# A layer on one Trainium2 core: VectorE's work in the 64 attention steps dealt out in another order, w_ada's rows mostly in the first 24 steps, the end of the stage reordered, half of x loaded again by SyncE

## The chip, the cores and the metric

The kernel runs on one core of one Trainium2 chip. The metric is the device time of one execution in microseconds (us); the figure compared is the median over runs. The engines have short names in all rows: PE is TensorE's matmul, PEld its weight load, DVE is VectorE, ACT is ScalarE, POOL is GpSimd and SP is SyncE, which here only issues DMAs. Every engine runs its own instructions in the order in which they are written, and waits on semaphores of the others.

## The reference

One transformer layer over 1024 tokens of width 1024, in f32. What matters here, cut short:

```python
mod = silu(c) @ w_ada + b_ada          # six parts of 1024: shift, scale, gate, twice
h = rmsnorm(x, g_mix) * (1 + scale) + shift
q, k, v, q_idx, k_idx, w_idx, u = split(h @ w_in)
# index attention, in query blocks of 128: every token takes its 256 best keys
score = sum_h w_idx[h] * relu(q_idx[h] . k_idx)      # causal
sel = top_k(score, 256)
o = softmax(q . k[sel] / 8) @ v[sel]                 # 8 heads of 64, 2 kv heads
# conformer branch: 31-tap depthwise convolution of 512 channels, layernorm over channels, silu
y = silu(layernorm(conv31(glu(u)) + conv_b) * norm_g + norm_b)
x = x + gate1 * (concat(o, y) @ w_out)
x = x + gate2 * mlp(rmsnorm(x) * (1 + scale2) + shift2)
out = rmsnorm(x, g_final)
```

## The kernel before

Each f32 matmul is made as three rounded ones (high x high, low x high, high x low), so nearly every operand is split into a `_hi` and a `_lo` part. The execution has this order: norm and first parts of `w_ada`; the projections with `w_in`; index scores; then the **attention stage**, which this change is about (338 to 707 us of the profiled execution); `w_out` (to 796 us); the MLP, over half of the whole time, which the change does not touch.

The attention stage is 64 **steps**, n = 8t + i for query block t (128 tokens) and head i. One list, `MICRO`, is written out by hand as Python tables, and all engines run through that same list, each taking from it what is its own. So the list sets the order on every engine. Per step there are: `scores` (PE, two heads at a time, matmuls into one of two banks), `mask` (DVE, adds the mask or the index selection and takes the maximum, line 1521 and two small rows behind it), `exp` (ACT), `turn` (PE transposes the probabilities, ACT copies them, line 1002), `values` (PE). PE's scores of a pair of heads overwrite the banks of the pair before and wait for its masks (line 2012 waits for line 1521). Once per query block: `invert` and `spread` (reciprocal of the softmax sums, turned by PE), `divide` (DVE, line 1558, frees the bank of `values`: PE's line 2090 of the next block waits for it), `out_hi` (ACT, line 1022) and `out_lo` (DVE, line 1561) which split the block's output.

Dealt out among these steps is other work:

- `topk` for query tile 4 (DVE, pairs at lines 1385 and 1387, steps 0 to 30). For tiles 5 to 7 the 256th best score is found by a search in rounds instead: `sel_pass` (ACT counts the scores above a candidate with three Sign activations, line 949), then `sel_step` (DVE, four small operations on 128x3 at lines 1406 to 1416, which give the next candidate). Rounds lie in steps 0 to 31 with n % 4 < 3; the pass of step n is answered by the `sel_step` of step n + 1. `sel_fin` (DVE, lines 1436 to 1454) finishes each tile in 6 steps between 32 and 51.
- convolution taps on PE, whose diagonal matrices POOL builds.
- the convolution's layernorm for the first 512 tokens (half 0), lines 1568 to 1594 on DVE and 1035 to 1048 on ACT: centre, square, sum (PE), root, reciprocal, scale, affine, sigmoid (`ln_gate`), silu, and the split `ln_hi` and `ln_lo`. Half 1 lies at the end of the stage.
- 32 rows of `w_ada` (`ada`, DVE, line 1542 or 1545): one 128x1024 operation each, from a buffer `raw` that SP fills. SP has 4 such buffers and issues the transfer for slot n when slot n - 4 has been used. The sums are needed by `modsum` (step 46) and `gate` (steps 57 and 58).
- at steps 60 and 62 and after the stage POOL splits the rows of `w_out` into high and low (lines 593 and 595).

Behind the stage, PE runs `w_out` in units: first on attention output and conv half 0 for tokens 0 to 511 (`mixed` in the list), then for the other 512 tokens, for which it needs `out_lo` of block 7 and then `ln_lo` of half 1. DVE adds the result to x (`mixed1`, lines 1608 and 1610), and ACT issues the DMAs that load x again.

## Time and profile before

| what | value |
|---|---|
| median of 3 runs | 2895.67 us |
| all runs | 2901.35, 2895.67, 2895.38 us |
| the profiled execution | 2891.27 us |
| its span, first to last instruction | 2889.5 us |
| mean granted clock of PE | 0.973 |
| PE busy | 2692.2 us, 93% of the span |
| DVE busy | 1673.8 us, 58% |
| POOL busy | 1148.5 us, 40% |
| ACT busy | 764.8 us, 26% |
| attention stage, starts of its steps | 0: 338.0, 8: 377.5, 16: 421.3, 24: 464.2, 32: 513.7, 48: 611.7, 63: 690.6 us |

Times are read from the start of the span. A step starts where its row of line 1521 starts on DVE. The profiled execution is 4.4 us below the median of the runs. Busy shares are averages over stages with different limits, so the stages are read one by one.

### The profile page before, as it was taken

The page shows a single profiled execution, that of the slowest core. Times are in us where ns is not written, and L with a number is a line of the kernel's source. Part 1 is how long each engine was busy: PE and PEld are TensorE (multiplying, and loading weights), DVE is VectorE, ACT ScalarE, POOL GpSimd, SP SyncE. Part 2 cuts the span into 40 slices and gives each one's busy share as a digit, 9 for nine tenths or more (in the row PEclk, how much of TensorE's full clock was granted, in tenths as well). Part 3 has the DMA queues.
Part 4 walks back from the last instruction along what each step waited for, and adds up shares of the span by engine and source line. Part 5 has one row for each costly group of instructions (what it writes and reads, how often), then busy time and mean ns, then how long its engine had stood idle before and what let it go on. Part 6 is the DMA issues. An engine that isn't in the chain of part 4 may idle for free.

```text
span 2889.5 us, 34826 instructions
## 1 busy us (share of the span) xinstructions
PE 2692.2 (93%) x13584; PEld 2213.7 (77%) x13584; DVE 1673.8 (58%) x2150; ACT 764.8 (26%) x1322; POOL 1148.5 (40%) x764
## 2 busy tenths in 40 slices
PE   4999898899999999999999999788799999999998
PEld 4867776677878888888877777677688888888887
DVE  6278988854666566566585782455526334444335
ACT  4235477434231001111023442222214100111002
POOL 2422464533554344344342223333264334334332
PEclk8999999999999999999999999999999999999999
DMA  6201111111411111111122110000221111111111
GB/s 217 66 12 34 36 61 58 59 38 36 147 59 46 42 58 46 41 58 44 48 73 73 37 37 15 1 1 1 87 95 59 39 49 58 37 50 58 36 51 59
DMA packets 142490, 153.35 MB, mean 53 GB/s; under 512 B 7183, under 2 KB 105252, under 8 KB 142374
## 3 DMA queue, kind: packets, MB, share of 16 engines
q1 hardware_dynamic: 136512, 141.87, 15.5%
q10 hardware_dynamic: 5862, 9.89, 1.0%
q8 instruction: 78, 1.28, 0.2%
q14 instruction: 38, 0.31, 0.0%
HBM read 143.35 MB, written 8.39 MB: 53 GB/s over the span
## 4 chain that ended last, share of the span: by engine, by line
PE 78%; DVE 13%; ACT 4%; issue 3%; DMA 1%; POOL 1%; ACTq 0%; SPq 0%; DVEq 0%; POOLq 0%
PE ps L1936 11%; PE ps L1921 11%; PE ps L1937 11%; PE ps L1938 11%; PE ps L1922 11%; PE ps L1923 11%; PE ps L2318 3%; PE ps L2012 2%; DVE yt L1758 2%; ACT sel_out L949 1%; PE ps L2090 1%; DVE yt L1747 1%; DVE score L1387 1%; PE ps L2116 1%; DVE best L1385 1%
## 5 line engine op out<-in xcount | busy, mean ns | idle before, releaser
L1921 PE MATMUL ps<-h_hi,w_hi 128*128 128x512 f32 x1472 | 585.4, 398 | 10.1 <-issue 5.6
L1922 PE MATMUL ps<-h_lo,w_hi 128*128 128x512 f32 x1472 | 575.6, 391 | 0.0
L1923 PE MATMUL ps<-h_hi,w_lo 128*128 128x512 f32 x1472 | 575.3, 391 | 0.0
L696 POOL TENSOR_TENSOR w_hi<-raw,zero 128x1024 fp32r<-128x1024 f32 x128 | 243.7, 1904 | 781.0 <-PE ps L1923 398.0
L1936 PE MATMUL ps<-w_hi,u_hi 128*128 128x512 f32 x1024 | 399.2, 390 | 0.0
L1937 PE MATMUL ps<-w_lo,u_hi 128*128 128x512 f32 x1024 | 399.1, 390 | 0.0
L1938 PE MATMUL ps<-w_hi,u_lo 128*128 128x512 f32 x1024 | 398.9, 390 | 0.0
L1078 ACT ACTIVATE act_r<-ps 128x512 f32<-128x512 f32 x128 | 76.5, 598 | 1131.4 <-PE ps L1923 1131.4
L1642 DVE TENSOR_TENSOR act_r<-act_r 128x512 f32<-128x512 f32 x128 | 166.0, 1297 | 330.4 <-ACT act_r L1078 330.4
L699 POOL TENSOR_TENSOR w_lo<-raw,w_hi 128x1024 fp32r<-128x1024 f32 x128 | 338.1, 2641 | 10.0
L1921 PEld LDWEIGHTS ps<-h_hi,w_hi 128*128 128x128 f32 x1472 | 278.0, 189 | 77.2 <-issue 17.0
L1922 PEld LDWEIGHTS ps<-h_lo,w_hi 128*128 128x128 f32 x1472 | 278.1, 189 | 59.9 <-issue 3.7
L1923 PEld LDWEIGHTS ps<-h_hi,w_lo 128*128 128x128 f32 x1472 | 277.9, 189 | 58.6
L1647 DVE TENSOR_TENSOR u_lo<-act_r,u_hi 128x512 fp32r<-128x512 f32 x128 | 226.8, 1781 | 0.0
L1936 PEld LDWEIGHTS ps<-w_hi,u_hi 128*128 128x128 f32 x1024 | 192.7, 188 | 40.0
L1938 PEld LDWEIGHTS ps<-w_hi,u_lo 128*128 128x128 f32 x1024 | 192.7, 188 | 40.0
L1937 PEld LDWEIGHTS ps<-w_lo,u_hi 128*128 128x128 f32 x1024 | 192.7, 188 | 40.0
L1655 DVE TENSOR_TENSOR x<-x,ps 128x512 f32<-128x512 f32 x128 | 88.0, 687 | 212.2 <-PE ps L1938 212.2
L1936 PE MATMUL ps<-w_hi,h_hi 128*128 128x512 f32 (+2 forms) x512 | 184.0, 359 | 18.2 <-DVE h_lo L1862 6.7
L1937 PE MATMUL ps<-w_lo,h_hi 128*128 128x512 f32 (+2 forms) x512 | 182.7, 357 | 0.0
L1938 PE MATMUL ps<-w_hi,h_lo 128*128 128x512 f32 (+2 forms) x512 | 182.3, 356 | 0.0
L1662 DVE TENSOR_TENSOR x<-x,tmp 128x512 f32<-128x512 f32 x128 | 155.0, 1211 | 4.4
(421 smaller groups left out, 4158.4 us busy)
## 6 DMA issues: line engine op xcount, KB each, us to landing
raw<-in_w_up_dram SPq DMA_DIRECT2D x64, 512.0 KB, 4.0
raw<-in_w_down_dram SPq DMA_DIRECT2D x64, 512.0 KB, 3.2
raw<-in_w_ada_dram SPq DMA_DIRECT2D x48, 512.0 KB, 3.7
raw<-in_w_in_dram SPq DMA_DIRECT2D x32, 512.0 KB, 3.7
raw<-in_w_out_dram SPq DMA_DIRECT2D x32, 512.0 KB, 3.3
x<-in_x_dram SPq DMA_DIRECT2D x8, 512.0 KB, 10.7
x<-in_x_dram ACTq DMA_DIRECT2D x8, 512.0 KB, 9.4
x_mid<-x SPq DMA_DIRECT2D x8, 512.0 KB, 5.4
```

What stands on the lines that cost most here:

```text
L696: g_.tensor_tensor(w_hi[:, r, :], raw[:, r, :], zero.to_broadcast([P, 1024]), ALU.add).then_inc(sem("w_hi_done"), 1)
L699: g_.tensor_tensor(w_lo[:, r, :], raw[:, r, :], w_hi[:, r, :].bitcast(F32), ALU.subtract).then_inc(sem("split_done"), 1)
L1642: v.tensor_tensor(act_r[:, b % 4, :], act_r[:, b % 4, :], act_r[:, b % 4, :], ALU.mult).then_inc(sem(f"u_sq{k}"), 1)
L1647: v.tensor_tensor(u_lo[c // 4][:, c % 4, :], act_r[:, c % 4, :], u_hi[c // 4][:, c % 4, :].bitcast(F32), ALU.subtract).then_inc(sem(f"u_lo ...
L1655: v.tensor_tensor(x[:, t, cols], x[:, t, cols], ps[:, n % 8, :], ALU.add).then_inc(sem(f"down_out{k}"), 1)
L1662: v.tensor_tensor(x[:, t, cols], x[:, t, cols], tmp2[:, n % 2, :], ALU.add).then_inc(sem(f"x_sum{k}"), 1)
L1921: mm(ps[:, bank, :], wh, h_hi[:, k, cols], start=(k == 0), stop=False)
L1922: mm(ps[:, bank, :], wh, h_lo[:, k, cols], start=False, stop=False)
L1923: last = mm(ps[:, bank, :], wl, h_hi[:, k, cols], start=False, stop=(k == NK - 1))
L1936: mm(o, hi[:, k0 + k, tok], wh, start=(start and k == 0), stop=False)
L1937: mm(o, hi[:, k0 + k, tok], wl, start=False, stop=False)
L1938: last = mm(o, lo[:, k0 + k, tok], wh, start=False, stop=(stop and k == 1))
```

## The change

Nothing is computed otherwise; instructions stand elsewhere in the engines' orders.

- **w_ada's rows** (`ADA_SLOTS`): before one row at steps 0, 1, 3, 4, 6, 8, 9, 11 and so on, to 49 (32 rows); now one in each of steps 0 to 23, then 25, 28, 39, 45, 46, 53, 54, 55.
- **divide, out_hi, out_lo** of block t - 1: from steps 8t + 3, 8t + 3, 8t + 4 to steps 8t + 2, 8t + 2, 8t + 3. On ACT `out_hi` then stands ahead of the three Sign activations of its step.
- **layernorm of half 0**: its four columns are dealt out over more steps (centre over 26 and 27, scale one each in 33 to 36, affine over 37 and 38, silu one each in 40 to 43); its reciprocal goes from 31 to 32.
- **sel_fin**: each tile one step later.
- **end of the stage, half 1**: square behind step 63's `exp`; sum, root later; reciprocal, scale and affine from before `invert` to behind `out_lo` of block 7.
- **x**: tiles 0 to 3 are loaded by SP, behind the transfer of the slot N_FIRST - 12 and a wait for the last scores (ahead of the later `w_out` slots), tiles 4 to 7 by ACT as before.

```diff
--- before.py
+++ after.py
@@ -399,7 +399,7 @@
         SEL_EARLY, SEL_ROUNDS = 8, 4
         SEL_AT = {n: SEL_EARLY + k for k, n in enumerate(n for n in range(32) if n % 4 < 3)}
         FIN_SLOTS = {}
-        for ti, at_slots in zip(SEL_TILES, (range(32, 38), range(39, 45), range(46, 52))):
+        for ti, at_slots in zip(SEL_TILES, (range(33, 39), range(40, 46), range(47, 53))):
             for part, n in enumerate(at_slots):
                 FIN_SLOTS[n] = [("sel_fin", ti, part)]
         UNIT_SLOTS = (0, 6, 12, 18, 24, 34, 42, 52, 62)
@@ -412,13 +412,17 @@
             return CONV_K * u + -(-CONV_K * (n - n0) // (n1 - n0))
 
         LN_BANK = (1, 7)
-        LN_SLOTS = {26: [("ln_mean", 0)], 28: [("ln_square", 0)], 29: [("ln_sum", 0)], 30: [("ln_root", 0)],
-                    31: [("ln_recip", 0)], 34: [("ln_scale", 0)], 37: [("ln_affine", 0)], 39: [("ln_gate", 0)],
-                    42: [("ln_silu", 0)], 62: [("ln_mean", 1), ("ln_square", 1)],
-                    63: [("ln_sum", 1), ("ln_root", 1), ("ln_recip", 1), ("ln_scale", 1), ("ln_affine", 1)]}
+        LN_SLOTS = {26: [("ln_mean", 0, 0), ("ln_center", 0, 0), ("ln_center", 0, 1)],
+                    27: [("ln_center", 0, 2), ("ln_center", 0, 3)],
+                    28: [("ln_square", 0, 0)], 29: [("ln_sum", 0, 0)], 30: [("ln_root", 0, 0)], 32: [("ln_recip", 0, 0)],
+                    33: [("ln_scale", 0, 0)], 34: [("ln_scale", 0, 1)], 35: [("ln_scale", 0, 2)], 36: [("ln_scale", 0, 3)],
+                    37: [("ln_affine", 0, 0), ("ln_affine", 0, 1)], 38: [("ln_affine", 0, 2), ("ln_affine", 0, 3)],
+                    39: [("ln_gate", 0, 0)], 40: [("ln_silu", 0, 0)], 41: [("ln_silu", 0, 1)], 42: [("ln_silu", 0, 2)],
+                    43: [("ln_silu", 0, 3)], 62: [("ln_mean", 1, 0)] + [("ln_center", 1, c) for c in range(NCC)],
+                    63: [("ln_square", 1, 0)]}
         HI_SLOTS = {44: 3, 46: 2, 54: 1, 62: 0}
         N_ADA = 4 * NK
-        ADA_SLOTS = {8 * i // 5: i for i in range(N_ADA)}
+        ADA_SLOTS = {n: i for i, n in enumerate(list(range(24)) + [25, 28, 39, 45, 46, 53, 54, 55])}
         GATE_SLOTS = {46: [("modsum", 0, 0)], 57: [("gate", 0, 0), ("gate", 0, 1)], 58: [("gate", 1, 0), ("gate", 1, 1)]}
         WSPLIT_SLOTS = {60: 0, 62: 1}
         MICRO = [("split_q", 0, 0), ("split_q", 1, 0)]
@@ -439,12 +443,12 @@
                     MICRO.append(("mask", t, i + e))
                     if n - 1 in SEL_AT:
                         MICRO.append(("sel_step", SEL_AT[n - 1], 0))
-                    if t and i + e == 4:
+                    if t and i + e == 2:
+                        MICRO.append(("divide", t - 1, 0))
+                    if t and i + e == 3:
                         MICRO.append(("out_lo", t - 1, 0))
                     if t and i + e == 0:
                         MICRO.append(("invert", t - 1, 0))
-                    if t and i + e == 3:
-                        MICRO.append(("divide", t - 1, 0))
                     if t and i + e == 1:
                         middle = (taps[1] + taps[2]) // 2
                         if middle > taps[1]:
@@ -457,11 +461,11 @@
                     if n in WSPLIT_SLOTS:
                         MICRO.append(("wsplit", WSPLIT_SLOTS[n], 0))
                     MICRO.append(("exp", t, i + e))
-                    if t and i + e == 3:
+                    if t and i + e == 2:
                         MICRO.append(("out_hi", t - 1, 0))
                     if n in HI_SLOTS:
                         MICRO += [("ln_hi", 0, HI_SLOTS[n]), ("ln_lo", 0, HI_SLOTS[n])]
-                    MICRO += [(kind, half, 0) for kind, half in LN_SLOTS.get(n, [])]
+                    MICRO += LN_SLOTS.get(n, [])
                     for ti, at_slots in TOPK_SLOTS.items():
                         if n in at_slots:
                             done, of = n - at_slots[0], len(at_slots)
...
-        MICRO += [("values", NT - 1, NH - 4), ("turn", NT - 1, NH - 2), ("mixed", 0, 0), ("turn", NT - 1, NH - 1),
-                  ("invert", NT - 1, 0), ("mixed", 0, 1), ("spread", NT - 1, 0), ("ln_gate", 1, 0), ("values", NT - 1, NH - 2), ("divide", NT - 1, 0),
-                  ("mixed", 0, 2), ("mixed", 0, 3), ("out_hi", NT - 1, 0), ("out_lo", NT - 1, 0), ("ln_silu", 1, 0)]
+        MICRO += [("values", NT - 1, NH - 4), ("turn", NT - 1, NH - 2), ("ln_sum", 1, 0), ("mixed", 0, 0),
+                  ("turn", NT - 1, NH - 1), ("invert", NT - 1, 0), ("ln_root", 1, 0), ("mixed", 0, 1), ("spread", NT - 1, 0),
+                  ("values", NT - 1, NH - 2), ("divide", NT - 1, 0), ("mixed", 0, 2), ("mixed", 0, 3), ("out_hi", NT - 1, 0),
+                  ("out_lo", NT - 1, 0), ("ln_recip", 1, 0)]
+        MICRO += [(kind, 1, c) for kind in ("ln_scale", "ln_affine") for c in range(NCC)] + [("ln_gate", 1, 0)]
+        MICRO += [("ln_silu", 1, c) for c in range(NCC)]
         MICRO += [("mixed", 1, t) for t in range(4)]
         MICRO += [(kind, 1, c) for c in reversed(range(NCC)) for kind in ("ln_hi", "ln_lo")]
 
...
+                if n == N_FIRST - 12:
+                    sp.wait_ge(sem("score_full"), NH * NT)
+                    for t in range(NT // 2):
+                        sp.dma_start(x[:, t, :], a["x"][0, t * P:(t + 1) * P, :]).then_inc(sem("x_in0"), 16)
 
             def mlp(k, n0, freed0, up, down):
 
@@ -1054,8 +1065,8 @@
 
             act.wait_ge(sem("attn_lo"), NT)
             act.wait_ge(sem("ln_silu"), 2 * NCC)
-            for t in range(NT):
-                act.dma_start(x[:, t, :], a["x"][0, t * P:(t + 1) * P, :]).then_inc(sem(f"x_in{t // 4}"), 16)
+            for t in range(NT // 2, NT):
+                act.dma_start(x[:, t, :], a["x"][0, t * P:(t + 1) * P, :]).then_inc(sem("x_in1"), 16)
 
             act.dma_start(frow, a["g_final"].rearrange("(o d) -> o d", o=1).to_broadcast([P, D])).then_inc(sem("frow_in"), 16)
 
@@ -1567,28 +1578,24 @@
                                          vec[:, m0 + 3 * NK:m0 + 5 * NK], ALU.add))
                     v.scalar_tensor_tensor(scl[:, 1, :], mod[:, 4 * NK:5 * NK], 1.0, vcols("g_mlp"), ALU.add,
                                            ALU.mult).then_inc(sem("scale_ready"), 1)
-                if kind == "ln_mean":
+                if kind == "ln_center":
                     dve.wait_ge(sem("ln_mean"), t + 1)
-                    for c in range(NCC):
-                        v.scalar_tensor_tensor(conv[:, c, cols], ps[:, LN_BANK[t], :], -1.0 / CONV_CH, conv[:, c, cols],
-                                               ALU.mult, ALU.add).then_inc(sem("ln_cent"), 1)
+                    v.scalar_tensor_tensor(conv[:, i, cols], ps[:, LN_BANK[t], :], -1.0 / CONV_CH, conv[:, i, cols],
+                                           ALU.mult, ALU.add).then_inc(sem("ln_cent"), 1)
                 if kind == "ln_recip":
                     dve.wait_ge(sem("ln_sd"), t + 1)
                     link(v.reciprocal(tmp2[:, 1, :], tmp2[:, 1, :]))
...
```

The first place is DVE in step 11, the fourth step of query block 1. Before:

```order
L1521 ISA prob,smax<-ps,cmask 128x256
L1521 ISA smax 128x1
L1528 TENSOR_SCALAR snm<-smax 128x1
L1406 TENSOR_TENSOR sel_acc<-sel_sum,sel_rank 128x3
L1407 TENSOR_TENSOR sel_pick<-sel_acc,sel_cand 128x3
L1408 TENSOR_TENSOR sel_low<-sel_low,sel_pick 128x3
L1416 SCALAR_TENSOR_TENSOR sel_cand<-sel_base,sel_low 128x3
L1558 TENSOR_TENSOR otok<-ps,otok 128x512
L1385 MAX best<-score_161 128x8
L1387 MATCH_REPLACE score_161<-best,score_161 128x640
L1542 SCALAR_TENSOR_TENSOR gate_sum_174<-raw,csil,gate_sum_174 128x1024
L1521 ISA prob,smax<-ps,cmask 128x256
```

And now:

```order
L1532 ISA prob,smax<-ps,cmask 128x256
L1532 ISA smax 128x1
L1539 TENSOR_SCALAR snm<-smax 128x1
L1417 TENSOR_TENSOR sel_acc<-sel_sum,sel_rank 128x3
L1418 TENSOR_TENSOR sel_pick<-sel_acc,sel_cand 128x3
L1419 TENSOR_TENSOR sel_low<-sel_low,sel_pick 128x3
L1427 SCALAR_TENSOR_TENSOR sel_cand<-sel_base,sel_low 128x3
L1569 TENSOR_TENSOR otok<-ps,otok 128x512
L1396 MAX best<-score_161 128x8
L1398 MATCH_REPLACE score_161<-best,score_161 128x640
L1553 SCALAR_TENSOR_TENSOR shift_sum<-raw,csil,shift_sum 128x1024
L1532 ISA prob,smax<-ps,cmask 128x256
```

The second of these begins at step 10's mask and ends at step 11's: `divide` (`otok<-ps,otok`) has gone from behind the small operations on 128x3 of step 11 to behind those of step 10, and the step has got a row of `w_ada` (`raw,csil`) as step 11 has.

The second place is ACT in step 10, the three Sign activations (`sel_out,sel_sum`) and the copy `h_hi<-otok`. Before:

```order
L1010 ACTIVATE prob,ssum<-prob,snm 128x256
L949 ACTIVATE sel_out,sel_sum<-score_162,sel_cand,sel_sign 128x768
L949 ACTIVATE sel_out,sel_sum<-score_163,sel_cand,sel_sign 128x896
L949 ACTIVATE sel_out,sel_sum<-score_164,sel_cand,sel_sign 128x1024
L1002 ACTIVATE probT<-ps 128x256
L1028 ACTIVATE conv<-ps,vec 128x512
L1010 ACTIVATE prob,ssum<-prob,snm 128x256
L1022 ACTIVATE h_hi<-otok 128x4x128
```

And now:

```order
L1021 ACTIVATE prob,ssum<-prob,snm 128x256
L1033 ACTIVATE h_hi<-otok 128x4x128
L960 ACTIVATE sel_out,sel_sum<-score_162,sel_cand,sel_sign 128x768
L960 ACTIVATE sel_out,sel_sum<-score_163,sel_cand,sel_sign 128x896
L960 ACTIVATE sel_out,sel_sum<-score_164,sel_cand,sel_sign 128x1024
L1013 ACTIVATE probT<-ps 128x256
L1039 ACTIVATE conv<-ps,vec 128x512
L1021 ACTIVATE prob,ssum<-prob,snm 128x256
```

The copy, which waits for DVE's `divide`, stood behind step 11's exp and now stands ahead of step 10's Sign activations.

The third place is DVE at steps 42 to 44, where block 4's output is divided, half 0's silu is made (`conv<-conv,squares`) and tile 6 is finished (`sel_out`, score_163). Before:

```order
L1590 TENSOR_TENSOR conv<-conv,squares 128x512 x4
L1447 TENSOR_SCALAR sel_out<-score_163,sel_kth 128x896
L1448 SCALAR_TENSOR_TENSOR sel_out<-ones,sel_out 128x896
L1521 ISA prob,smax<-ps,score_162 128x768
L1521 ISA smax 128x1
L1528 TENSOR_SCALAR snm<-smax 128x1
L1558 TENSOR_TENSOR otok<-ps,otok 128x512
L1450 TENSOR_SCALAR sel_out<-sel_out,sel_ties 128x896
L1451 SCALAR_TENSOR_TENSOR sel_out<-score_163,sel_kth,sel_out 128x896
L1542 SCALAR_TENSOR_TENSOR gate_sum_175<-raw,csil,gate_sum_175 128x1024
L1521 ISA prob,smax<-ps,score_162 128x768
```

And now:

```order
L1569 TENSOR_TENSOR otok<-ps,otok 128x512
L1597 TENSOR_TENSOR conv<-conv,squares 128x512
L1454 TENSOR_SCALAR sel_out<-score_163,sel_kth 128x896
L1455 TENSOR_REDUCE sel_higher<-sel_out 128x1
L1456 TENSOR_SCALAR sel_ties<-sel_higher 128x1
L1532 ISA prob,smax<-ps,score_162 128x768
L1532 ISA smax 128x1
L1539 TENSOR_SCALAR snm<-smax 128x1
L1572 TENSOR_TENSOR h_lo<-otok,h_hi 128x4x128
L1597 TENSOR_TENSOR conv<-conv,squares 128x512
L1458 TENSOR_SCALAR sel_out<-score_163,sel_kth 128x896
L1459 SCALAR_TENSOR_TENSOR sel_out<-ones,sel_out 128x896
```

Step 42 had four rows of silu and the first two rows of a part of `sel_fin`; now one silu row stands in each step, with one part of `sel_fin` and no row of `w_ada`.

The fourth place is DVE's end of the stage, behind the last mask. Before:

```order
L1528 TENSOR_SCALAR snm<-smax 128x1
L1577 RECIPROCAL tmp_151<-tmp_151 128x512
L1580 TENSOR_TENSOR conv<-conv,tmp_151 128x512 x4
L1585 TENSOR_SCALAR conv<-conv,vec 128x512 x4
L1554 RECIPROCAL srec<-ssum 128x8
L1558 TENSOR_TENSOR otok<-ps,otok 128x512
L1561 TENSOR_TENSOR h_lo<-otok,h_hi 128x4x128
L1590 TENSOR_TENSOR conv<-conv,squares 128x512 x4
L1594 TENSOR_TENSOR h_lo<-conv,h_hi 128x512 x4
```

And now:

```order
L1539 TENSOR_SCALAR snm<-smax 128x1
L1565 RECIPROCAL srec<-ssum 128x8
L1569 TENSOR_TENSOR otok<-ps,otok 128x512
L1572 TENSOR_TENSOR h_lo<-otok,h_hi 128x4x128
L1587 RECIPROCAL tmp_151<-tmp_151 128x512
L1589 TENSOR_TENSOR conv<-conv,tmp_151 128x512 x4
L1593 TENSOR_SCALAR conv<-conv,vec 128x512 x4
L1597 TENSOR_TENSOR conv<-conv,squares 128x512 x4
L1601 TENSOR_TENSOR h_lo<-conv,h_hi 128x512 x4
```

The reciprocal, scale and affine of half 1 stood ahead of the reciprocal of the softmax sums (`srec<-ssum`), and now stand behind `h_lo<-otok,h_hi`.

## Rows read from the trace of the kernel before

**Rows 1.** Windows: us; busy PE, PEld, DVE, ACT, POOL; granted clock; DMA share; GB/s.

```profile
338.00:464.20 126.20, 113.72 (x599) 87.44 (x598) 103.97 (x240) 89.51 (x187) 79.02 (x92) 0.93 0.20 63
464.20:508.40 44.20, 35.99 (x198) 25.13 (x196) 36.98 (x82) 36.16 (x67) 16.79 (x19) 0.93 0.15 49
508.40:679.60 171.20, 156.13 (x1117) 123.90 (x1117) 111.74 (x185) 73.24 (x143) 78.33 (x78) 0.94 0.14 44
679.60:705.10 25.50, 20.94 (x153) 14.73 (x154) 13.55 (x21) 13.27 (x22) 1.24 (x1) 0.97 0.06 22
705.10:800.80 95.70, 90.87 (x439) 75.66 (x437) 60.28 (x57) 28.81 (x46) 57.80 (x31) 0.98 0.36 127
```

**Rows 2.** Waits of PE, 338 to 708 us: us in total, times, longest.

```profile
PE ps L2012 <- DVE smax L1521: 25.6, 9, 5.0
PE ps L2090 <- DVE otok L1558: 6.1, 3, 3.3
PE ps L2098 <- DVE srec L1554: 2.3, 1, 2.3
PE ps L2135 <- ACT squares L1035: 2.2, 1, 2.2
```

**Rows 3.** The same view, 508.4 to 679.6 us.

```profile
PE ps L2012 <- DVE smax L1521: 19.4, 6, 5.0
```

**Rows 4.** Timeline of PE, three stalls: start, busy, row, in brackets the wait before.

```profile
508.37 0.79 PE L2012 MATMUL ps<-k_hi,q_hi 64*128 64x512 f32 x2 [5.03 <-DVE smax L1521]
...
576.96 0.76 PE L2012 MATMUL ps<-k_hi,q_hi 64*128 64x512 f32 x2 [4.97 <-DVE smax L1521]
...
591.05 0.80 PE L2012 MATMUL ps<-k_hi,q_hi 64*128 64x512 f32 x2 [4.07 <-DVE smax L1521]
```

**Rows 5.** Window behind the stall at 577 us, as in rows 1.

```profile
577.00:580.40 3.40, 3.40 (x24) 3.06 (x26) 3.33 (x4) 1.55 (x3) 0.22 (x1) 0.51 0.00 0
```

**Rows 6.** Timeline of DVE in steps 3 to 6.

```profile
357.26 1.28 DVE L1542 SCALAR_TENSOR_TENSOR gate_sum<-raw,csil,gate_sum 128x1024 f32<-128x1024 f32 x1
...
363.26 0.77 DVE L1406 TENSOR_TENSOR sel_acc<-sel_sum,sel_rank 128x3 f32<-128x3 f32 x1 [0.95 <-ACT sel_out L949]
...
369.75 0.70 DVE L1406 TENSOR_TENSOR sel_acc<-sel_sum,sel_rank 128x3 f32<-128x3 f32 x1 [1.63 <-ACT sel_out L949]
```

**Rows 7.** Timeline of ACT and DVE around steps 10 and 11.

```profile
389.81 1.03 ACT L949 ACTIVATE sel_out<-score,sel_cand,sel_sign 128x768 f32<-128x768 f32 x1 [0.66 <-DVE sel_cand L1416]
...
396.69 0.69 DVE L1558 TENSOR_TENSOR otok<-ps,otok 128x512 f32<-128x512 f32 x1
...
397.41 0.63 ACT L1022 ACTIVATE h_hi<-otok 128x512 fp32r<-128x512 f32 x1 [2.40 <-DVE otok L1558]
```

**Rows 8.** Groups of DVE by line, 338 to 508.4 us: busy, mean ns, idle before.

```profile
L1407 DVE TENSOR_TENSOR sel_pick<-sel_acc,sel_cand 128x3 f32<-128x3 f32 x23 | 11.4, 497 | 0.8
...
L1406 DVE TENSOR_TENSOR sel_acc<-sel_sum,sel_rank 128x3 f32<-128x3 f32 x24 | 7.4, 306 | 15.8 <-ACT sel_out L949 15.8
```

**Rows 9.** Timeline of DVE in steps 31 and 42.

```profile
510.34 3.35 DVE L1577 RECIPROCAL tmp<-tmp 128x512 f32<-128x512 f32 x1
...
567.67 3.77 DVE L1590 TENSOR_TENSOR conv<-conv,squares 128x512 f32<-128x512 f32 x4
```

**Rows 10.** Timeline of DVE and POOL behind the last mask.

```profile
698.85 2.50 DVE L1580 TENSOR_TENSOR conv<-conv,tmp 128x512 f32<-128x512 f32 x4
...
707.91 1.05 POOL L593 CAST w_hi<-raw 128x1024 fp32r<-128x1024 f32 x1 [27.06 <-PE ps L2090]
...
711.91 8.57 DVE L1590 TENSOR_TENSOR conv<-conv,squares 128x512 f32<-128x512 f32 x4
...
744.85 0.69 DVE L1608 TENSOR_TENSOR tmp<-ps,gate 128x512 f32<-128x512 f32 x1 [6.37 <-PE ps L1938]
```

**Rows 11.** DMA issues of the page: KB each, median us from issue to landing.

```profile
raw<-in_w_ada_dram SPq DMA_DIRECT2D x48, 512.0 KB, 3.7
...
x<-in_x_dram ACTq DMA_DIRECT2D x8, 512.0 KB, 9.4
```

19 lines of the change are left out of this document (8 added, 11 removed).

## Prediction

> **What bounds the kernel now.** I read the windows first, cut at the places where the stage changes its limit [rows 1]. From 338 to 464 us (steps 0 to 23) PE is busy 113.7 of 126.2 us, but DVE 104.0 and ACT 89.5 as well: none is full. In this stretch ACT and DVE hand the search for tiles 5 to 7 to each other: DVE waits 15.8 us in all for ACT's counts [rows 8], ACT waits for the next candidate (0.66 us, [rows 7]). That loop sets the pace; PE follows. From 464 to 508 us (steps 24 to 31) PE is busy 36.0 of 44.2 us, DVE 37.0. From 508 to 680 us PE is busy 156.1 of 171.2 us and DVE only 111.7: there PE is the bound, and what it loses is worth looking for. The end, 680 to 705 us, and `w_out` to 801 us are PE's too (90.9 of 95.7).
>
> The chain of losses is in the waits of PE [rows 2]: 25.6 us in nine waits of the scores for a mask. Of these 19.4 us in six waits lie from 508.4 us on [rows 3], but the first of the six is the one that ends at 508.37 (5.03 us, [rows 4]); so the PE-bound stretch itself holds 14.4 us in five, the largest 4.97 and 4.07 us [rows 4]. DVE has a mean load of 65% there, so the masks are late because single steps hold too much, not because DVE has too much work. A second loss is the clock. The stretch has a mean granted clock of 0.94 [rows 1], 10.3 us of 171.2. Right behind the stall of 4.97 us, from 577.0 to 580.4 us, the clock is 0.51, the 1.2 GHz level instead of 2.4, with PE busy all the time [rows 5]: 3.4 us there do 1.7 us of work. So a stall costs its own time and then 1.7 or 3.4 us more.
>
> The Trainium skill, "TensorE: Matmul & The Clock Gate" (Part 1), says that activity of PE is what keeps its fast clock and idleness what loses it; by this rule too removing stalls pays twice, and the trace agrees by the row of 0.51 behind the stall.
>
> **The change, step by step.** *Steps 0 to 23.* Nine rows of `w_ada` come in, 1.28 us each [rows 6]. Where a row stands in the step ahead, DVE waits 0.95 us for ACT's count, where none stands 1.63 us [rows 6]; a row of 1.28 us fits into the 1.63. This holds for the six steps 2, 5, 10, 13, 18 and 21: nothing. Steps 7 and 15 have no pass behind them, nothing waits there, and the row lies on the loop: 2.6 us. Step 23 likewise, 1.3 us, but PE's waits of about the same length that end there go (I take 1.1 off for lateness that PE already has). *Divide and out_hi.* ACT's copy takes 0.63 us and, ahead of the Sign activations of steps 10 and 18, waits for a `divide` of 0.69 us that follows DVE's small operations [rows 7]: about 1.3 us each time, 2.6 together. `divide` in one step and `out_lo` in the next take each other's place on DVE: nothing. That is 2.6 + 1.3 + 2.6 - 1.1 = 5.4; the loop has about 1.2 us of slack in these three periods, ACT's own 0.66 us wait [rows 7] being part of it, so I take **+4.2 us** at step 24, bounds 1.5 (only steps 7 and 15, a half hidden) and 15.4 (below). PE's 6.1 us of waits for `divide` [rows 2] lie inside this stretch and are worth nothing while the loop sets the pace.
>
> *Steps 24 to 31.* Rows leave steps 24, 27 and 30; that of step 30 stands directly ahead of mask 31, for which PE waits 5.03 us [rows 4]: **-1.3 us**. The third `out_hi` move (step 26) and centre cut in two take about as much as they give. So PE's scores of step 32 start at 508.4 + 4.2 - 1.3 = 511.3 us. A reciprocal of 3.35 us [rows 9] goes from ahead of mask 32 to ahead of mask 33, where PE has a pair of steps of 8 us or more to cover it.
>
> *Steps 32 to 61.* Before, single steps hold four silu rows, 3.77 us [rows 9], and behind them a part of `sel_fin` and a row of `w_ada`; the third place of the change shows them gone from one step into four. I laid the new order of DVE beside PE's own work per pair of steps (8 to 12 us at full clock, 171.2 - 14.4 - 10.3 = 146.5 in all): all masks but one come ahead of PE; the one of step 45 comes 1.8 us late, behind `sel_fin`'s last part and a row of `w_ada`. Left are this 1.8 us, 1.7 of clock behind it and 1.0 of clock behind the stall of step 31: 4.5 us instead of 24.7. **-20.2 us**, bounds -10 (half of the stalls stay as shorter ones that still cost the clock) and -24.
>
> *End of the stage.* Before, the reciprocal of 3.35 us and eight more rows stand ahead of `invert`, and PE waits 2.3 us for `srec` [rows 2]; now nothing stands there: -2.3. The 2.2 us wait for the squares [rows 2] moves with `ln_sum` behind more of PE's work, but the squares start behind step 63's `exp`: +0.3. Sum **-2.0**, bounds 0 and -4. The work moved behind `out_lo` runs beside POOL's splits, which start at 707.9 us, when `pv_done` comes [rows 10]. There four rows take 8.57 us, where four like them take 2.50 us alone [rows 10]. Priced so: reciprocal 3.4 [rows 9], scale, silu and lo 8.6 each, affine 2.5, together 31.7 us, from about 708 us on, with some 2 us of waits for the Sigmoids: DVE is through at 742 us on the clock of before. PE needs it for the second half of `w_out`, which by half of the last window [rows 1] begins at about 751; before, DVE had 6.4 us to spare ahead of 744.85 [rows 10]. With DVE's first `mixed1` rows between, it keeps 4 us or more. Cost nothing; without that cover up to 8 us.
>
> *DMAs.* A `w_ada` transfer takes 3.7 us, a tile of x 9.4 in the median [rows 11]. In steps 0 to 23 a row is used every 5.3 us with four buffers, so it lands in time. x's first half starts some 15 us earlier, on SP, with `w_out`'s slots behind it; PE wants the first of those only at about 715 us. Nothing.
>
> The sum: +4.2 - 1.3 - 20.2 - 2.0 = -19.3. The profiled execution of 2891.27 us would become 2872; it lies 4.4 us below the median of the runs, so against 2895.67 us I say **2876 us**.
>
> **The rivals.** *A: the rows land on the loop.* If DVE's wait for ACT doesn't take them up (a row in step n delays mask n + 1, that its exp, that the next pass), nine rows of 1.28 and three copies of 1.3 cost 15.4 us: 11.2 more, -8, **2888 us**. For it: ACT and DVE are both over 70% busy. Against it: a wait of 1.63 turned into 0.95 where a row stands. Chance 0.13. *B: the end of the stage pays.* All moved DVE rows at 2.14 us each (8.57/4) beside POOL, the reciprocal slowed as well, end about 8 us past PE's need: -11, **2884 us**. For it the 8.57 us; against it 4 us or more of slack. Chance 0.12. The Trainium skill, "SBUF — State Buffer", section "SBUF: two separate sides", says that VectorE and GpSimd share a port pair that one of them holds for a whole instruction. [...] *C, slower: the search's small rows.* In steps 0 to 31 the rows of line 1407 take 497 ns in the mean [rows 8], and single ones 0.16 or 0.77 [rows 6]: beside POOL they are five times as long. If the added DVE rows shift them so that all meet POOL's diagonals, a `sel_step` of four rows goes from 1.5 to 3.0 us, 24 times on the loop: +35, net +15, **2911 us**. It decides from 0.8 us per `sel_step`. Against it: POOL's order isn't changed, and 63% of its time there is busy already. Chance 0.06. *D: the stalls only move.* If DVE is late anyway through the 4.2 us by which steps 0 to 23 end later, or PE's waits shift to other masks with the clock as low, the stretch gains 5 instead of 20: about **2892 us**. Against it: 35% of DVE idle there, in long pieces. Chance 0.12.
>
> **How the numbers follow.** Chances: forecast 0.57, A 0.13, B 0.12, D 0.12, C 0.06. With its bounds the forecast covers 2868 to 2884. To hold eight in ten the range reaches from 2866 to 2891: it takes in A, B and most of the bounds, leaves out D's upper half and C. A difference under 0.2% (5.8 us) is about what this measurement can't tell from none. Faster by more (under 2889.9): forecast, B, most of A, a part of D: 0.80. Within: the rest of A and D, 0.13. Slower: C and a tail of D, 0.07.
>
> **What would show it.** Right: step 24 starts at 467 to 469 us; PE's waits for line 1521's successor from there to step 61 sum to under 4 us, and the clock of that stretch is 0.97 or more; scores of step 62 start 16 to 18 us earlier; no wait for `srec`; PE without a gap from there to 780 us. Wrong: step 24 at 475 or later (A), 490 (C); waits of PE for `h_lo` or `x` past 740 us (B); waits for masks above 10 us in new places (D). The number that I trust least is the +4.2, since it sums small terms of a loop of two engines.

## The result

The changed kernel takes 2890.44 us in the median of 20 runs (2885.75 to 2892.92), the kernel before 2897.46 in 20 runs (2891.8 to 2901.35): a ratio of 0.9976, with an interval of 0.997 to 0.9983, so 7 us faster. I had said 2876, almost 20 us faster. The profiled execution took 2888.07 us, with a span of 2886.3.

First the windows of the changed kernel, cut at the same steps as those of before [rows 1]:

```profile
338.00:471.50 133.50, 116.17 (x615) 87.75 (x613) 119.62 (x248) 89.19 (x187) 85.48 (x94) 0.96 0.29 91
471.50:512.90 41.40, 31.25 (x180) 21.07 (x180) 32.75 (x79) 33.65 (x63) 14.73 (x17) 0.99 0.12 39
512.90:675.70 162.80, 152.05 (x1119) 121.49 (x1119) 107.21 (x179) 74.64 (x146) 78.07 (x78) 0.96 0.06 20
675.70:698.00 22.30, 19.85 (x151) 13.81 (x152) 5.97 (x12) 12.44 (x22) 0.68 (x1) 1.00 0.38 142
698.00:793.10 95.10, 90.27 (x445) 75.10 (x439) 73.66 (x66) 29.78 (x47) 58.69 (x31) 0.99 0.31 105
```

Steps 0 to 23 have become 7.3 us longer, 24 to 31 2.8 shorter, the PE-bound stretch 8.4 shorter, and the end and `w_out` 3.8 shorter. The first cut behind steps 0 to 23 is the mask of step 24, and that mask now starts 6.3 us behind PE's scores of step 24 instead of 2.4; measured from scores to scores, as in the table below, steps 0 to 23 cost 3.6 us and steps 24 to 31 1.1. In the third row PE is busy 4 us less, the clock is 0.96 instead of 0.94; it is the right kind of gain, less than half as large as forecast.

PE's waits, 338 to 712 us, and then from 512.95 to 675.8 us alone (compare [rows 2, 3]):

```profile
PE ps L2019 <- DVE smax L1532: 28.1, 14, 4.3
...
PE ps L2142 <- ACT squares L1046: 1.7, 1, 1.7
PE ps L2105 <- DVE srec L1565: 1.3, 1, 1.3
...
PE ps L2019 <- DVE smax L1532: 13.8, 7, 4.3
```

Over the whole stage the waits for masks have grown, 28.1 us in fourteen for 25.6 in nine. As before, one of the seven is the stall that ends at the stretch's start. The timeline of PE shows it and the larger ones behind it (line 2019 is what 2012 was):

```profile
512.89 0.80 PE L2019 MATMUL ps<-k_hi,q_hi 64*128 64x512 f32 x2 [4.03 <-DVE smax L1532]
...
543.97 0.49 PE L2019 MATMUL ps<-k_hi,q_hi 64*128 64x512 f32 x2 [1.29 <-DVE smax L1532]
...
573.88 0.51 PE L2019 MATMUL ps<-k_hi,q_hi 64*128 64x512 f32 x2 [0.60 <-DVE smax L1532]
...
586.61 0.50 PE L2019 MATMUL ps<-k_hi,q_hi 64*128 64x512 f32 x2 [4.27 <-DVE smax L1532]
...
622.41 0.50 PE L2019 MATMUL ps<-k_hi,q_hi 64*128 64x512 f32 x2 [2.13 <-DVE smax L1532]
...
642.41 0.51 PE L2019 MATMUL ps<-k_hi,q_hi 64*128 64x512 f32 x2 [1.24 <-DVE smax L1532]
```

The stall of 4.97 us [rows 4] is gone, as forecast (0.6 is left of it). That ahead of mask 45 is 4.27 instead of the forecast 1.8, and masks 37, 51 and 55 are late where the forecast had nothing.

**How the stage is compared.** The 2,090 us behind the stage are the same work in all kernels and differ by up to 7 us between profiles, as shown at the end, and the median of before moved by 2.6 us from one set of runs to another. So besides the runs I compare the starts of PE's rows: the scores of steps 0, 24, 32 and 62 and the first MLP matmul. A second profile of before (e5) repeats such lengths within 1 us, and its waits for masks too (26.5 us in nine). All in us: the lengths are differences of those starts, "PE idle" is the sum of PE's pauses over 0.3 us in the stage, "slow clock" the time in it with the granted clock at its lower level, "behind" the time from the first MLP matmul to the end of that profile; each row but the ratio comes from one profile. The ratio is that of the runs. e8 and e9 leave out most of the convolution's values:

| kernel | 0 to 24 | 24 to 32 | 32 to 62 | 62 to MLP | stage | PE idle | slow clock | behind | ratio to before, interval |
|---|---|---|---|---|---|---|---|---|---|
| before | 130.5 | 46.6 | 171.2 | 121.2 | 469.6 | 46.1 | 56.5 | 2088.7 | |
| e5_before_again | 131.5 | 46.6 | 171.2 | 121.1 | 470.4 | 47.0 | 56.5 | 2089.1 | |
| after | 134.1 | 47.7 | 162.8 | 117.3 | 461.9 | 46.4 | 31.8 | 2093.3 | 0.9976, 0.997 to 0.9983 |
| e1_rows_only | 133.1 | 46.5 | 169.0 | 121.2 | 469.9 | 46.8 | 49.4 | 2092.9 | 1.0004, 0.9995 to 1.0014 |
| e2_steps_only | 131.1 | 45.5 | 172.1 | 121.1 | 469.9 | 48.6 | 53.1 | 2088.8 | 0.9998, 0.9989 to 1.0008 |
| e3_rows_back | 127.7 | 47.9 | 174.1 | 117.4 | 467.1 | 49.6 | 40.2 | 2088.5 | 0.9969, 0.9957 to 0.998 |
| e4_end_back | 133.2 | 47.7 | 164.4 | 121.2 | 466.5 | 45.6 | 42.9 | 2091.4 | 0.9981, 0.9971 to 0.999 |
| e6_divide_back | 133.6 | 44.7 | 162.0 | 117.4 | 457.7 | 40.6 | 37.7 | 2087.4 | 0.9945, 0.9929 to 0.9962 |
| e7_x_back | 134.0 | 47.6 | 162.8 | 117.4 | 461.8 | 46.5 | 31.8 | 2093.2 | 0.9978, 0.9968 to 0.9988 |
| e8_quiet_after | 117.4 | 44.4 | 158.1 | 117.3 | 437.2 | 27.6 | 23.9 | 2087.4 | 0.9872, 0.9855 to 0.9888 |
| e9_quiet_before | 114.1 | 45.8 | 164.3 | 121.0 | 445.1 | 31.5 | 34.7 | 2086.8 | one run |
| e10_copy_late | 132.4 | 47.3 | 164.4 | 117.4 | 461.4 | 42.9 | 38.2 | 2093.5 | 0.9958, 0.9944 to 0.9972 |
| e11_lo_later | 134.1 | 43.8 | 157.9 | 116.9 | 452.7 | 36.2 | 32.3 | 2093.0 | 0.9938, 0.9916 to 0.9961 |
| e12_rows_spread | 129.1 | 44.3 | 162.3 | 117.4 | 453.1 | 36.4 | 36.5 | 2088.5 | 0.9938, 0.9919 to 0.9956 |
| e13_spread_lo | 129.2 | 45.2 | 155.9 | 116.9 | 447.1 | 33.0 | 29.8 | 2088.3 | 0.9932, 0.9919 to 0.9944 |
| e14_fin_early | 130.0 | 45.2 | 155.1 | 116.8 | 447.2 | 30.6 | 32.8 | 2088.6 | 0.9907, 0.9893 to 0.9922 |

The columns of idle time and slow clock hold the most telling reading of the result. **PE is idle as long in the changed kernel's stage as in that of before**, 46.4 against 46.1 us: 4.0 us less in steps 32 to 61 (10.3 for 14.3) and 2.1 less at the end, and 6.5 more in steps 0 to 31 (28.8 for 22.3). What became shorter is PE's busy time, as the sums of the windows over the stage show, before and after:

```profile
sum 469.60, PE 422.50 PEld 330.71 DVE 332.25 ACT 246.16 POOL 236.66; mean PE 105.62 PEld 82.68 DVE 83.06 ACT 61.54 POOL 59.17
```

```profile
sum 461.90, PE 414.45 PEld 323.03 DVE 344.92 ACT 244.89 POOL 241.03; mean PE 103.61 PEld 80.76 DVE 86.23 ACT 61.22 POOL 60.26
```

The same matmuls take 8 us less, and the slow clock fell from 56.5 to 31.8 us of the stage. Those 24.7 us at half speed can be worth 12.4 at most, and less where they lie in pauses; in steps 32 to 61 the two fit (8.0 us less of slow clock, PE busy 4.1 us less). Over the table's sixteen rows the stage without PE's idle time grows by 0.37 us for each us of slow clock, with a correlation of 0.94. Stalls over 2 us ahead of the MLP became six instead of eleven (4.03 and 4.27 the longest), and shorter pauses took their place. The ten kernels with the new end have 0.0 to 2.6 us of slow clock from 62 to the MLP, where their lengths lie within 0.6 us; so small differences of stage length are read with the idle time beside them.

### The profile page after: what moved, and what is told of

Its sections match the earlier page's. It is cut to its first block, busy times and chain, and to the rows that moved or that the text cites. A ratio compares the mean times of both kernels' runs of the same rounds, so it can differ in the third digit from the quotient of the medians.

```text
span 2886.3 us, 34827 instructions
## 1 busy us (share of the span) xinstructions
PE 2687.2 (93%) x13584; PEld 2207.5 (76%) x13584; DVE 1686.2 (58%) x2150; ACT 763.3 (26%) x1322; POOL 1153.8 (40%) x764
## 4 chain that ended last, share of the span: by engine, by line
PE 77%; DVE 13%; ACT 5%; issue 4%; DMA 1%; POOL 1%; ACTq 0%; SPq 0%; DVEq 0%; POOLq 0%
PE ps L1943 11%; PE ps L1944 11%; PE ps L1928 11%; PE ps L1945 11%; PE ps L1930 11%; PE ps L1929 11%; PE ps L2325 4%; ACT sel_out L960 2%; DVE yt L1765 2%; PE ps L2019 1%; DVE score L1398 1%; DVE yt L1754 1%; DVE best L1396 1%; PE ps L2097 1%; PE ps L1911 1%
## 5 line engine op out<-in xcount | busy, mean ns | idle before, releaser
L1928 PEld LDWEIGHTS ps<-h_hi,w_hi 128*128 128x128 f32 x1472 | 278.0, 189 | 77.3 <-issue 17.3
```

The lines of the kernel that those rows point to most:

```text
L1928: mm(ps[:, bank, :], wh, h_hi[:, k, cols], start=(k == 0), stop=False)
```

## The experiments

### One part alone, or taken back

e1 is the kernel before with one line (and the layernorm's columns written one by one, in the order of before):

```diff
-        ADA_SLOTS = {8 * i // 5: i for i in range(N_ADA)}
+        ADA_SLOTS = {n: i for i, n in enumerate(list(range(24)) + [25, 28, 39, 45, 46, 53, 54, 55])}
```

> The kernel before with only the new places of w_ada's rows. Theory 1 (the gain of the changed kernel in steps 32 to 61 comes from taking rows of w_ada out of them, and is paid for by 4.5 us in steps 0 to 31): PE's scores of step 32 start at about 512 us (3 to 4 us late), the stall ahead of mask 45 (4.07 us) falls below 2, that ahead of mask 43 (4.97 us) stays since no row stands in step 42, and the stretch from there to the scores of step 62 is 6 to 8 us shorter than in the kernel before: in all -3 us. Theory 2 (the gain comes from dealing out the layernorm and sel_fin, rows matter little there): the stretch is at most 3 us shorter, and the kernel is 1 us slower to 1 us faster.

Stage +0.3 us: steps 0 to 23 pay 2.6 (1.6 against the second profile of before), the stretch from 32 gains 2.2. The stall ahead of mask 43 stays at 4.99 us, as theory 1 has it, that of mask 45 falls to 2.46. The size is nearer to theory 2.

e2 is the kernel before with half 0's layernorm and `sel_fin` as changed (`LN_SLOTS` 26 to 43 and `FIN_SLOTS` of the diff), all else as before.

> The kernel before with only half 0 of the layernorm dealt out over more steps and sel_fin one step later; rows of w_ada, divide, end of the stage and x as before. Theory 1: the stall of 4.97 us ahead of mask 43 goes, but the rows in steps 40, 41, 43 and 44 keep mask 45 late by 4 us or more; the stretch from step 32 to 62 is 2 to 4 us shorter, -3 us in all. Theory 2: the stretch is 6 us or more shorter, and with nothing lost in steps 0 to 31 the kernel gains 6 to 8 us, as much as the whole change does.

Both theories fail by their sizes: the stage is 0.3 us longer. What theory 1 said of the masks holds. The stalls ahead of masks 37 and 45:

```profile
545.80 0.80 PE L2013 MATMUL ps<-k_hi,q_hi 64*128 64x512 f32 x2 [5.16 <-DVE smax L1526]
...
593.15 0.79 PE L2013 MATMUL ps<-k_hi,q_hi 64*128 64x512 f32 x2 [5.89 <-DVE smax L1526]
```

The 4.97 us ahead of mask 43 went and came back elsewhere: dealt out, the silu rows lie in steps 40, 41 and 43, beside rows of `w_ada` that still stand there.

e3 is the changed kernel with the first line of e1's diff.

> The changed kernel with w_ada's rows where they were before. Theory 1: steps 0 to 31 get their 3.5 to 4.5 us back (scores of step 32 at about 509 us), the stretch from 32 to 62 loses 4 to 6 us; the kernel is 0 to 2 us slower than the changed one. Theory 2: steps 0 to 31 get it back and the stretch loses at most 2 us: the kernel is 2 to 4 us faster than the changed one, 9 to 11 faster than before.

Against the changed kernel the stage is 5.2 us longer by the profile; steps 0 to 23 get 6.4 us back (127.7), but the stretch from 32 to 62 is 174.1 us, longer than before. The 6.4 us are not the price of nine rows alone: PE's idle time there is 2.6 us less, and the slow clock 10.2 us instead of 17.1. The runs say 2887.52 us, a ratio not told apart from the changed kernel's. In the one profile the part behind the stage is 4.8 us shorter (2088.5 for 2093.3), which makes up for the stage; why, and whether the other runs have it too, stays open. Neither theory had these sizes. With e1 and e2: **the two parts only gain together**, -9.2 us in that stretch (e6 below, which has both, against before) where alone they give -2.2 and +0.9.

e4 is the changed kernel with the end of the stage in the old order (`LN_SLOTS` 62 and 63 and the `MICRO` lines behind the loop).

> The changed kernel with the end of the stage in its order of before. The profile of the changed kernel shows 3.9 us gained from the scores of step 62 to the first MLP matmul, 1.3 in the wait for srec (half as long, not gone), 0.5 in the wait for the squares and the rest in a slow clock of 3.4 us that no longer stands there. If the order does this: the kernel is 3 to 4 us slower than the changed one. Rival (the order only moves the waits, and the clock's slow stretch fell there by chance): at most 2 us slower.

3.9 us come back from 62 to MLP (121.2), the old waits of 2.23 and 2.34 us with them, and 0.7 more elsewhere. The order does this: the six profiles with the old end have 121.0 to 121.2 us there, the ten with the new one 116.8 to 117.4. The runs don't show it: 2891.01 us is a ratio of 0.9981, 1.5 us from the changed kernel and inside its interval, where 3 to 4 us were expected. (My text above takes the wait of 1.3 us for `srec` for the end's; it is the one at 472.5 us, ahead of step 25's `spread`. At the end the changed kernel has none.)

e6 is the changed kernel with these three places back:

```diff
-                    if t and i + e == 2:
-                        MICRO.append(("divide", t - 1, 0))
-                    if t and i + e == 3:
+                    if t and i + e == 4:
                         MICRO.append(("out_lo", t - 1, 0))
...
                         MICRO.append(("invert", t - 1, 0))
+                    if t and i + e == 3:
+                        MICRO.append(("divide", t - 1, 0))
...
-                    if t and i + e == 2:
+                    if t and i + e == 3:
                         MICRO.append(("out_hi", t - 1, 0))
```

> The changed kernel with divide, out_hi and out_lo in their steps of before. Of the 7 us of the change the rows of w_ada alone give nothing (their own kernel 2 us slower than before, the changed one 3 us faster without them), the dealt-out steps alone nothing, and the end 1 to 4. Theory 3: the rest is this move, since PE's line for values of the next block waited for divide (6.1 us in three waits, each followed by a slow clock); then this kernel is 3 to 5 us slower than the changed one. The prediction's view (those waits lie under the search loop, and out_hi ahead of the Sign activations costs 1.3 us at each of steps 10, 18 and 26): this kernel is 1 to 3 us faster than the changed one.

Theory 3 falls. The kernel is 2880.01 us, by the ratios 9 us faster than the changed one, with intervals that don't meet. The stage is 4.2 us shorter; in the profile the part behind it is 5.9 us shorter too. Of the 4.2 us 3.0 lie in steps 24 to 31 and 0.8 behind, where the stall of 2.13 us ahead of mask 51 is gone: `divide` (0.69 us) no longer stands in step 50 with the scan of `sel_fin`, and the scan no longer meets GpSimd's split of q (2.37 us instead of 3.01, see the last section). The prediction had 3.9 us for the three copies ahead of the Sign activations; PE's idle time is 5.8 us less.

> The changed kernel with all of x loaded by ACT's queue as before. The prediction's view (the load is hidden): within 1 us of the changed kernel. Rival (the first mixed rows wait for x, which now comes behind the silu of half 1, later than before): 1 to 3 us slower, with a wait of DVE for x_in in its rows.

e7 has the diff's two places on x back. Stage within 0.1 us: the load is hidden, as forecast.

### What makes the masks late

e8 and e9 let GpSimd do almost nothing in the instructions that build the convolution's diagonals, so most of the convolution's values are left out; its splits of q and of `w_out` stay as they are:

```diff
-                                        g.tensor_tensor(dst[:, d % 2, 0:taps, :],
-                                                        ident.unsqueeze(1).to_broadcast([P, taps, P]), col,
-                                                        ALU.mult).then_inc(sem("diag_ready"), 1)
+                                        few = slice(0, 2 if d >= 2 else P)
+                                        g.tensor_tensor(dst[:, d % 2, 0:taps, few],
+                                                        ident.unsqueeze(1).to_broadcast([P, taps, P])[:, :, few],
+                                                        col[:, :, few], ALU.mult).then_inc(sem("diag_ready"), 1)
```

> The changed kernel, in which GpSimd writes only 2 of 128 columns of every diagonal matrix from the third on, so that the convolution's values are left out and its rows of 128x512 to 128x2048 become short; all instructions and waits stay. Theory 4 (what keeps the masks late is DVE's rows made long beside GpSimd, 0.16 to 0.77 us, 0.62 to 1.32 us): steps 0 to 31 become 8 us or more shorter, the stalls ahead of masks 45 (4.27 us) and 51 (2.13 us) fall by half or more, and the kernel is 12 us or more faster. Rival (the order of DVE's rows and ACT's passes set the pace, GpSimd costs little): at most 4 us faster, and the stalls stay.

The stage is 24.7 us shorter, 16.7 of it in steps 0 to 23, and the kernel 31 us faster (2859.26): GpSimd's diagonals do slow the stage, as theory 4 has it. Of its two stalls the one ahead of mask 45 falls to 1.89 us, that of mask 51 doesn't. Groups of DVE there (busy, mean ns), the changed kernel:

```profile
L1418 DVE TENSOR_TENSOR sel_pick<-sel_acc,sel_cand 128x3 f32<-128x3 f32 x17 | 8.8, 516 | 0.6
L1417 DVE TENSOR_TENSOR sel_acc<-sel_sum,sel_rank 128x3 f32<-128x3 f32 x17 | 7.7, 451 | 8.7 <-ACT sel_out L960 8.7
L1419 DVE TENSOR_TENSOR sel_low<-sel_low,sel_pick 128x3 f32<-128x3 f32 x17 | 7.3, 431 | 0.6
...
L1427 DVE SCALAR_TENSOR_TENSOR sel_cand<-sel_base,sel_low 128x3 f32<-128x3 f32 x16 | 4.4, 277 | 0.6
```

and e8:

```profile
L1418 DVE TENSOR_TENSOR sel_acc<-sel_sum,sel_rank 128x3 f32<-128x3 f32 x17 | 2.8, 163 | 12.0 <-ACT sel_out L961 12.0
L1419 DVE TENSOR_TENSOR sel_pick<-sel_acc,sel_cand 128x3 f32<-128x3 f32 x17 | 2.8, 162 | 0.6
L1420 DVE TENSOR_TENSOR sel_low<-sel_low,sel_pick 128x3 f32<-128x3 f32 x17 | 2.7, 161 | 0.6
L1428 DVE SCALAR_TENSOR_TENSOR sel_cand<-sel_base,sel_low 128x3 f32<-128x3 f32 x16 | 2.6, 162 | 0.6
```

28.2 us against 10.9 for operations on 3 elements a lane: 17.3 us less, beside 16.7 us of stretch. Not all of it need be gained there, since DVE waits 3.3 us longer for ACT (12.0 for 8.7) and its wider rows shrink too. So the mechanism of rival C is real and large, but it was in the kernel before as well (28.3 us of such rows, 10.9 in e9). The 1.89 us ahead of mask 45 are the 1.8 of the prediction's ledger; the stall of mask 51 (2.98) has a scan beside a split of q ahead of it, which this edit leaves in place. The Trainium skill, "SBUF — State Buffer" (section "SBUF: two separate sides"), says that a VectorE operation with two SBUF inputs, or in a 2-port mode, and a GpSimd operation that reads SBUF share a port pair, which the one that starts first holds for its whole instruction. The four rows have two inputs each and agree: 0.16 us with the diagonals short, 0.28 to 0.52 in the mean beside rows of GpSimd of 0.94 us.

> The kernel before, in which GpSimd writes only 2 of 128 columns of every diagonal matrix from the third on (the convolution's values are left out). With the same done to the changed kernel, PE's scores of step 32 to step 62 took 158.1 us instead of 162.8, and the step 45 stall was 1.9 us, the 1.8 that the prediction had for it. Theory 4 (GpSimd's share in what is left of the changed kernel's stalls is why it gained 8 us there instead of 20): here that stretch is 168 us or more, so that without GpSimd the change would gain 10 us or more in it against 8.4 with it. Rival (GpSimd costs both orders alike): the stretch is 163 to 167 us, the change gains as much without it as with it, and the prediction's 20 fails for another reason.

Theory 4, as put here, falls: with the diagonals short the change gains 6.2 us in that stretch (164.3 to 158.1), with them long 8.4. They cost the old order 6.9 us there and the new one 4.7, and are no reason for the missing 12 us. Nor is it why the added rows cost what they do in steps 0 to 23: quiet, the change loses 3.3 us there, with GpSimd 2.6 to 3.6.

> The changed kernel with divide in step 8t + 2, but out_hi behind step 8t + 3's exp and out_lo in step 8t + 4, as before. With all three back the stage was 4.2 us shorter. Theory 5 (the cost is ACT's: the copy and its wait for divide stand ahead of the Sign activations): this kernel has the 4 us as well, with 44.7 us instead of 47.7 from step 24 to 32. Rival (the cost is DVE's: divide in a step that has a scan or a centre beside it): it has none of it, and the stall of 2.13 us ahead of mask 51 stays.

e10 is the changed kernel with out_hi at `i + e == 3` and out_lo at `i + e == 4`. It lies between the two theories. By the stage it has almost none of the 4 us (461.4; steps 24 to 31 take 47.3 us, not theory 5's 44.7), but 6.4 us more of slow clock fell into it. PE's idle time is 42.9 us, 3.5 less than in the changed kernel and 2.3 more than with `divide` back too (40.6); the runs go the same way, 5 us faster than the changed kernel (0.0018 of 2897), with intervals that just touch, where e6 is 9 us faster. The 3.5 us are 1.3 in steps 0 to 23, 1.3 in 24 to 31 and 0.8 behind, where no Sign activation stands. So at most 2.6 are the copies' ahead of the Sign activations, of the 3.9 that the prediction had for three; e10 moves `out_lo` on DVE as well, so that ACT's share isn't isolated. The 2.3 are `divide`'s own place on DVE, which the prediction had at nothing: 2.6 less in steps 24 to 31 and 0.7 less behind, where mask 51's stall of 2.13 us stays in e10 and goes in e6, against 0.9 more in steps 0 to 23.

In steps 42 to 45 DVE runs all but without a pause in the changed kernel:

```profile
573.83 1.17 DVE L1572 TENSOR_TENSOR h_lo<-otok,h_hi 128x512 fp32r<-128x512 f32 x1
574.93 1.32 DVE L1597 TENSOR_TENSOR conv<-conv,squares 128x512 f32<-128x512 f32 x1
576.17 1.25 DVE L1458 TENSOR_SCALAR sel_out<-score,sel_kth 128x896 f32<-128x896 f32 x1
577.45 2.02 DVE L1459 TENSOR_TENSOR_SCAN sel_out<-ones,sel_out 128x896 f32<-128x896 f32 x1
...
582.28 0.83 DVE L1601 TENSOR_TENSOR h_lo<-conv,h_hi 128x512 fp32r<-128x512 f32 x1 [1.62 <-ACT h_hi L1059]
583.03 1.25 DVE L1461 TENSOR_SCALAR sel_out<-sel_out,sel_ties 128x896 f32<-128x896 f32 x1
584.31 1.15 DVE L1462 SCALAR_TENSOR_TENSOR sel_out<-score,sel_kth,sel_out 128x896 f32<-128x896 f32 x1
```

The only pause, in step 44, is a wait for ACT's `ln_hi` that stands in the same step: DVE is the late engine and waits for one that it holds up itself (ACT does `exp` of that step first, which waits for DVE's mask). e11 is e6 with

```diff
-                        MICRO += [("ln_hi", 0, HI_SLOTS[n]), ("ln_lo", 0, HI_SLOTS[n])]
+                        MICRO += [("ln_hi", 0, HI_SLOTS[n])]
+                    if n - 1 in HI_SLOTS:
+                        MICRO += [("ln_lo", 0, HI_SLOTS[n - 1])]
```

> The changed kernel with divide, out_hi and out_lo back, and each ln_lo of half 0 one step behind its ln_hi. Theory 6 (DVE's wait of 1.62 us for ACT's ln_hi in step 44 is most of what the prediction's ledger left out of the stall of 4.26 us ahead of mask 45): that stall falls to 2.6 us or less, the wait goes, and the stretch from step 32 to 62 is 2 to 3.5 us shorter than the 162.0 with ln_lo in place. Rival (the wait only covers rows that GpSimd slows anyway, or mask 47 takes the stall over): less than 1 us.

```profile
581.43 0.50 PE L2021 MATMUL ps<-k_hi,q_hi 64*128 64x512 f32 x2 [2.31 <-DVE smax L1534]
```

Theory 6 holds by the profile: the stall is 2.31 instead of 4.26 us, mask 55's 1.25 is gone too, and the stretch is 157.9 instead of 162.0. The runs (2879.85 us, ratio 0.9938) are not told apart from e6's; in this profile the part behind the stage is 5.6 us longer.

### Towards a better order

e12 is e6 with rows of `w_ada` where DVE waited for PE, and no longer in steps 7, 15 and 23, which lay on the search loop:

```diff
+        ADA_SLOTS = [n for n in range(23) if n not in (7, 15)] + [25, 28, 39, 41, 41, 47, 49, 53, 57, 57, 57]
...
+                    MICRO += [("ada", k, 0) for k in range(N_ADA) if ADA_SLOTS[k] == n]
```

> The changed kernel with divide, out_hi and out_lo back, and w_ada's rows in steps 0 to 22 but 7 and 15, then 25, 28, 39, 41 (two), 47, 49, 53 and 57 (three), where DVE waited for PE. By the prediction's price for rows that lie on the search loop steps 0 to 23 become 3.9 us shorter (steps 7, 15 and 23 at 1.3 each), by the 6.4 us that nine added rows cost in the run with the rows back 2.1; steps 45 and 54 without rows take 1.3 us each off the stalls of masks 47 and 55, which PE shows as 1.25 at most. So 3 to 5 us faster than with divide back alone. Rival (PE or ACT bounds steps 7 and 15 too, and the loop only waits longer elsewhere): under 1.5 us.

Steps 0 to 23 are 129.1 us, 4.5 shorter than e6's: the price of 1.3 us for each of the three steps holds (3.9 for 4.5). Steps 32 to 61 lose nothing. The runs, 0.9938 for e6's 0.9945, don't tell the two apart. e13 has e11's and e12's edits.

> Both edits together: divide, out_hi and out_lo back, w_ada's rows spread as in the run before, ln_lo one step behind ln_hi. If what they took away stands apart (4.5 us of the stage by the rows in steps 0 to 23, 4.1 by ln_lo in steps 32 to 61), the stage is about 449 us long and the kernel 2871 to 2874 us, 4 to 5 us faster than with either. Rival (they overlap, as the added rows and the dealt-out steps did): under 2 us.

The stage is 447.1 us: they add, and later `ln_lo` shortens the stretch once more, from e12's 162.3 to 155.9. The runs (2875.45) show less of it than the profile: 2871 to 2874 was expected, and the ratio is not told apart from e12's. e14 moves tile 6's `sel_fin` out of the steps around `divide` (and the row of step 39 to 40):

```diff
-            for part, n in enumerate(at_slots):
+            for part, n in enumerate((39, 40, 41, 42, 44, 45) if ti == 6 else at_slots):
...
-                    33: [("ln_scale", 0, 0)], 34: [("ln_scale", 0, 1)], 35: [("ln_scale", 0, 2)], 36: [("ln_scale", 0, 3)],
+                    33: [("ln_scale", 0, 0)], 34: [("ln_scale", 0, 1), ("ln_scale", 0, 2)], 35: [("ln_scale", 0, 3)],
```

> The same, and tile 6's sel_fin in steps 39, 40, 41, 42, 44, 45, so that the step of divide holds no part of it, half 0's second and third scale both in step 34, and the row of step 39 in step 40. Theory 7 (each stall left is the sum of DVE's rows of the two steps ahead of an odd mask, so that it can be read off the list): the stall ahead of mask 45 (2.3 us) goes, that ahead of mask 37 (1.6) halves, and the stage is 2.5 to 4 us shorter than in the kernel without this. Rival (the stall moves on to mask 43, which then has 3.3 us more of sel_fin ahead of it): less than 1 us.

PE's waits from 510.4 to 665.5 us:

```profile
PE ps L2020 <- issue: 2.6, 1, 2.6
...
PE ps L2020 <- DVE smax L1533: 1.3, 2, 1.0
PE ps L2106 <- ACT probT L1014: 0.8, 1, 0.8
```

The 13.8 us in seven waits for masks are 1.3 in two, besides one of 2.6 us that the profile puts to nobody, at the stretch's start where the other kernels wait for mask 31. PE's idle time in the stage is 2.4 us less than e13's, the stretch only 0.8 us shorter and the stage no shorter. The stall ahead of mask 45 went down from 2.3 to 1.0, that of mask 37 (1.6) is gone, and two pauses of 0.9 for GpSimd's diagonals came up in steps 37 and 43: theory 7 holds for the masks, its 2.5 to 4 us for the stage's length do not. It has the lowest median of the kernels that compute everything, 2869.70 us, 27 us faster than before and about 20 than the changed one; its interval overlaps e13's.

## Why the prediction was wrong

- **Steps 32 to 61, the term of -20.2 us: this is the step that failed.** It measured -8.4: of the 24.7 us of loss 16.7 are left, 10.3 of idle PE (forecast 1.8) and 6.4 of clock (forecast 2.7; 12.9 us at half speed). "All masks but one come ahead of PE; the one of step 45 comes 1.8 us late" was worked out from the durations of DVE's rows alone, with nobody waited for. What the runs put in its place: a wait of DVE for ACT's `ln_hi` in step 44 and its like in 54 (4.1 us of the stretch, e11), and `divide` in one step with the scan of tile 7 (0.8, e6). e13 and e14, with rows and `sel_fin` parts moved as well, come to 155.9 and 155.1 us; against my 151.0 the last 4 us stay unexplained. These shares are read from one profile of each kernel. GpSimd's diagonals slow these rows, and made 1.89 into 4.27 us ahead of mask 45, but they cost the old order's stretch at least as much (e9), so they explain the stall and not the missing gain.
- **Steps 24 to 31, a second step that failed.** I had -1.3, with the third `out_hi` move and the split centre cancelling each other; +1.1 was measured. With `divide`, `out_hi` and `out_lo` back it is -1.9 (44.7 us, e6), so this move costs 3.0 us there.
- **Rivals.** D (stalls only move, 2892) came nearest: part of them moved. It was priced at 5 us of gain in the stretch; 8.4 were measured, and the waits for masks from step 24 to 61 sum to 16.2 us where I had under 4. A had 15.4 us in steps 0 to 23, where 3.6 were measured; B's wait of PE past 740 us didn't come. C's mechanism costs about 17 us, in both kernels; the change didn't add to it.
- **Steps 0 to 23.** +4.2 forecast, +3.6 measured, but not by its terms alone. The rows had 2.8 us of it and cost 2.6 (e1), and the price of 1.3 us for steps 7, 15 and 23 held (e12: 4.5 for 3.9). The copies had 1.4 behind the slack and cost 0.5 to 1.0 (against e6 and e1). With the rows in their old places the same move makes the stretch 3.4 us shorter (e3 against e2: 127.7 for 131.1) by 10 us less of slow clock, so that the number came near in part by luck. PE's 6.1 us of waits for `divide` are gone, and this stretch is no shorter for it, as forecast. (The 0.16 us of the search's small rows stand in e8's lines, not in [rows 6].)
- **The end.** -2.0 forecast, -3.9 measured (e4): `srec` gave 2.3, the squares 0.5, and the old order's 5.3 us of slow clock there are 1.0. The moved rows are hidden, as forecast: DVE's last `ln_lo` row ends at 732.2, I had 742, and no wait of PE follows. That is in part two errors against each other: no run shows the 2.5 us for the affine beside POOL, which took 7.51, while scale, silu and split took 6.39, 5.53 and 4.77 instead of 8.6 each. (Half of the last window is 753, not 751.)
- **x, DMAs.** Hidden (e7).

The moved rows of half 1 beside GpSimd:

```profile
704.16 3.35 DVE L1587 RECIPROCAL tmp<-tmp 128x512 f32<-128x512 f32 x1
707.54 6.39 DVE L1589 TENSOR_TENSOR conv<-conv,tmp 128x512 f32<-128x512 f32 x4
713.85 7.51 DVE L1593 TENSOR_SCALAR conv<-conv,vec 128x512 f32<-128x512 f32 x4
721.28 5.53 DVE L1597 TENSOR_TENSOR conv<-conv,squares 128x512 f32<-128x512 f32 x4
727.51 4.77 DVE L1601 TENSOR_TENSOR h_lo<-conv,h_hi 128x512 fp32r<-128x512 f32 x4 [0.70 <-ACT h_hi L1059]
732.20 0.68 DVE L1615 TENSOR_TENSOR tmp<-ps,gate 128x512 f32<-128x512 f32 x1
```

## What to carry to other kernels

When rows of an engine are laid out by hand beside another's, list for every row also whom it waits for: a split whose second half stands in the step of its first made the late engine wait for one that it delays, and moving it one step later gave 4 us of the stage's profile. Two edits that empty the same steps have to be priced as a pair: here each alone gave nothing, and both took 9 us off the stretch that they empty. Look at where PE's idle time went before you look at a span: it had only moved, and the gain came with less time at the lower clock. An operation of 0.16 us in a loop between two engines deserves as close a look as one of 3 us if a third engine can hold it up.

## What was not expected of the hardware

The affine rows read one SBUF tensor and took 7.51 us for four while GpSimd was busy with its splits for 7.35 us of them, where four in step 37 of the kernel before took 1.90 with no GpSimd row beside them. Not only rows with two inputs are held up, then. The row of before, and its window:

```profile
542.18 1.90 DVE L1585 TENSOR_SCALAR conv<-conv,vec 128x512 f32<-128x512 f32 x4
```

```profile
542.18:544.08 1.90, 1.86 (x16) 1.68 (x18) 1.90 (x6) 0.92 (x2) 0.00 (x0) 0.69 0.89 254
```

A scan is held up as well. Over 128x1024 it took 2.29 us in the kernel before with no GpSimd row beside it, 3.01 us in the changed kernel beside a split of q, and 3.26 us in e8, where the diagonals are short but the same split stands beside it:

```profile
619.18 2.29 DVE L1448 TENSOR_TENSOR_SCAN sel_out<-ones,sel_out 128x1024 f32<-128x1024 f32 x1
```

```profile
592.88 1.62 POOL L618 TENSOR_TENSOR q_lo<-qT,q_hi 128x512 fp32r<-128x512 f32 x1
...
593.38 3.26 DVE L1460 TENSOR_TENSOR_SCAN sel_out<-ones,sel_out 128x1024 f32<-128x1024 f32 x1
```

So a trial that shortens one kind of GpSimd row doesn't free DVE of the others. And the clock can stay at its lower level with PE at work, for a time that differs between kernels at the same matmuls. Windows of the changed kernel in the second half, and of before at the same matmuls:

```profile
1792.00:1816.00 24.00, 17.14 (x66) 14.69 (x66) 5.09 (x9) 3.30 (x6) 6.06 (x6) 0.50 0.00 1
```

```profile
1795.60:1806.00 10.40, 6.97 (x28) 5.98 (x28) 1.46 (x3) 0.60 (x1) 6.88 (x6) 0.51 0.00 0
1806.00:1820.00 14.00, 8.70 (x53) 7.61 (x54) 4.24 (x8) 2.83 (x5) 1.77 (x2) 0.88 0.01 1
```

24 us at half speed against about 14 of 24: the part behind the stage is 2093.3 us long in the one profile and 2088.7 in the other, a difference of more than half of what the change gains. The second profile of before has 2089.1, and by the table's column e1, e7, e10 and e11 have the long form, the others the short one or, e4, 2091.4. What decides between them isn't known.
